# GpSimd computes half of the key-times-query products of the decode attention

## What is computed

```python
def diff_attn_sample(q, k_new, v_new, k_past, v_past, lam):
    ...
    s_past = jnp.einsum('bqhcd,bshcd->bhcqs', q, k_past, preferred_element_type=jnp.float32) * scale
    ...
    w = diff_combine(jnp.concatenate([s_past, s_new], axis=-1), lam).astype(v_new.dtype)
    return (jnp.einsum('bhqs,bshe->bqhe', w[..., :P], v_past)
            + jnp.einsum('bhqs,bshe->bqhe', w[..., P:], v_new))
```

## Time and profile before

| | us |
|---|---|
| median of 3 runs | 1510.65 |
| lowest and highest | 1507.95, 1510.95 |
| the profiled execution, its time | 1508.39 |
| its span in the profile | 1506.6 |
| attention stage, from the first key product of turn 0 to that of turn 7 and its end | 728.3 to 928.2, 956.8 |
| busy in the span: TensorE, VectorE, ScalarE, GpSimd | 1321.3, 858.7, 533.0, 21.3 |

### The profile page before, as it was taken

The page is one execution under the profiler, slowest core; times in us unless marked ns, Lnnn a source line. Parts: engine busy times, 40 slices in busy tenths (PEclk is TensorE's granted clock), DMA queues, the critical chain, the costliest instruction groups (busy, mean ns, idle before and its releaser), DMA issues.

```text
span 1506.6 us, 19271 instructions
## 1 busy us (share of the span) xinstructions
PE 1321.3 (88%) x7150; PEld 975.0 (65%) x7150; DVE 858.7 (57%) x1101; ACT 533.0 (35%) x613; POOL 21.3 (1%) x26
## 2 busy tenths in 40 slices
PE   4797788999999979898669988877898999999976
PEld 1795555888888866797223222236546888888864
DVE  1436553666666602745888999476506666666334
ACT  1433224555555503442111111122216555555321
POOL 2000010000000000000000000000100000000000
PEclk9899888999999988999757887979658999999988
DMA  9937612999999692555439878964006999999300
GB/s 335 386 126 291 223 56 91 351 335 335 338 334 335 228 376 72 193 187 180 168 132 339 305 270 310 327 215 167 1 0 244 337 341 332 342 337 341 122 2 29
DMA packets 143713, 355.32 MB, mean 236 GB/s; under 512 B 4706, under 2 KB 4899, under 8 KB 143652
## 3 DMA queue, kind: packets, MB, share of 16 engines
q1 hardware_dynamic: 142388, 350.91, 65.6%
q0 software_dynamic: 1264, 3.59, 0.8%
HBM read 351.20 MB, written 3.28 MB: 235 GB/s over the span
## 4 chain that ended last, share of the span: by engine, by line
PE 72%; DVE 18%; issue 4%; ACT 2%; SPq 2%; DMA 2%; ACTq 0%; POOL 0%; DVEq 0%
PE gu L615 23%; PE pj L386 20%; PE pj L634 15%; PE tb L420 4%; DVE wring L1791 4%; DVE tokB L1794 3%; PE tb L417 2%; PE gu L452 2%; PE pj L781 2%; DMA wring<-in_a_w_in 1%; SPq L878 1%; PE pj L486 1%; PE tb L558 1%; DVE wlo L1419 1%; DVE xT L1460 1%
## 5 line engine op out<-in xcount | busy, mean ns | idle before, releaser
L1646 DVE TENSOR_TENSOR wlo<-wring,whi 128x2048 fp32r<-128x2048 f32 x128 | 290.1, 2289 | 103.3 <-ACT whi L1198 103.3
L1198 ACT ACTIVATE whi<-wring 128x2048 fp32r<-128x2048 f32 x128 | 244.5, 1914 | 143.8 <-PE gu L615 143.8
L634 PEld LDWEIGHTS pj<-tokB,wring 128*128 128x128 f32 x2048 | 233.5, 192 | 4.8 <-issue 2.1
L634 PE MATMUL pj<-tokB,wring 128*128 128x128 f32 x2048 | 234.0, 275 | 1.7 <-issue 1.7
L615 PE MATMUL gu<-whi,xhi 128*128 128x512 f32 x512 | 207.2, 405 | 12.9 <-DVE xlo L1672 12.9
L1094 ACT ACTIVATE reg<-pj 128x264 f32<-128x264 f32 (+3 forms) x166 | 83.3, 509 | 365.0 <-PE pj L386 148.0
L615 PE MATMUL gu<-wlo,xhi 128*128 128x512 f32 x512 | 204.4, 399 | 0.0
L615 PE MATMUL gu<-whi,xlo 128*128 128x512 f32 x512 | 204.0, 398 | 0.0
L781 PE MATMUL pj<-wring,ws 128*8 128x512 f32 x256 | 127.7, 659 | 1.0 <-DVE lamx L1870 1.0
L615 PEld LDWEIGHTS gu<-whi,xhi 128*128 128x128 f32 x512 | 98.0, 191 | 36.0 <-DVE xlo L1672 7.9
L615 PEld LDWEIGHTS gu<-whi,xlo 128*128 128x128 f32 x512 | 97.9, 191 | 22.6
(11 more groups left out here) (288 smaller groups left out, 1711.9 us busy)
## 6 DMA issues: line engine op xcount, KB each, us to landing
wring<-in_moe_w_gate SPq DMA_DIRECT2D x32, 2048.0 KB, 9.1
wring<-in_moe_w_up SPq DMA_DIRECT2D x32, 2048.0 KB, 10.0
wring<-in_moe_w_down SPq DMA_DIRECT2D x32, 2048.0 KB, 9.1
wring<-in_ada_w SPq DMA_DIRECT2D x24, 2048.0 KB, 13.0
wring<-in_cache_k SPq DMA_DIRECT2D x64, 512.0 KB, 5.0
wring<-in_cache_v SPq DMA_DIRECT2D x64, 512.0 KB, 5.0
wring<-in_a_w_in SPq DMA_DIRECT2D x4, 2048.0 KB, 20.0
wring<-in_a_w_out SPq DMA_DIRECT2D x2, 2048.0 KB, 16.7
```

What stands on the lines that cost most here:

```text
L634: m = pe.matmul(bank[:, i * P:(i + 1) * P], w[:, k, f * P:(f + 1) * P], aT[:, k, :], start=(k == 0), stop=(k == FB - 1))
L1198: act.activation(whi[q], quarter(wring, q, s), ACT.Copy).then_inc(hi_ready, 1)
L1646: dve.tensor_tensor(quarter(wlo, q, s), quarter(wring, q, s), whi[q].bitcast(F32), ALU.subtract).then_inc(lo_ready, 1)
```

## The change

GpSimd gets a loop over the 8 sequences behind its last store. For each it waits until the query is spread, and then, for both slots k, until the slot is loaded; it multiplies the second half of the slot (pages 2 and 3 of the four) in place with the query and counts `product_ready`. VectorE no longer multiplies for q = 1; there it waits for `product_ready` and does the sum alone. Nothing else is changed: which slots are used, when they are given back, and the order on the other engines.

```diff
         keys_used = sem("keys_used")
+        product_ready = sem("product_ready")
...
             pool.dma_start(o["v_sample"].rearrange("b t h e -> (b t) (h e)"), tokA[0:NB, 2, :]).then_inc(stored["vs"], 16)
+            for s in range(NB):
+
+                pool.wait_ge(pj_evac, at[f"spread{s}"])
+                for k in range(2):
+                    slot, count = cache_slot("k", s, k)
+                    pool.wait_ge(slot_in[slot], at["cache_loads"][slot] + 16 * count)
+                    keys = wring[:, slot, 2 * D:4 * D].rearrange("p (g n) -> p g n", g=2)
+                    pool.tensor_tensor(keys, keys, qbc[:, s % 2:s % 2 + 1, :].to_broadcast([P, 2, D]),
+                                       ALU.mult).then_inc(product_ready, 1)
             clear(1)
...
                 keys = wring[:, slot, q * 2 * D:(q + 1) * 2 * D]
-                link(dve.tensor_tensor(keys.rearrange("p (g n) -> p g n", g=2), keys.rearrange("p (g n) -> p g n", g=2),
-                                       qbc[:, s % 2:s % 2 + 1, :].to_broadcast([P, 2, D]), ALU.mult))
+                if q == 0:
+                    link(dve.tensor_tensor(keys.rearrange("p (g n) -> p g n", g=2), keys.rearrange("p (g n) -> p g n", g=2),
+                                           qbc[:, s % 2:s % 2 + 1, :].to_broadcast([P, 2, D]), ALU.mult))
+                else:
+
+                    dve.wait_ge(product_ready, 2 * s + k + 1)
```

## The result

The changed kernel took 1529.08 us (median of 5 runs, 1519.17 to 1531.09) against 1510.65 before, 1.0123 times as long (95% interval 1.0102 to 1.0144).

The account below looks back on a forecast made before the run. TensorE bounds nearly all, VectorE the key-score stage. Turn 0 6.1 slower, turns 1, 2 to 6 and 7 faster by 3.4, 2.5 and 1.5: -1.3 from 1508.4, 1507.1; at the runs' median 1509 us, range 1485 to 1526.

Parts of the forecast that it names:

- the gain without contention: Whole stage, if GpSimd and VectorE cost each other nothing: 14.6 us faster, 1496; as a rival, chance 0.27.
- GpSimd's price of 4.4 us: Each GpSimd product of 2048 columns takes 4.4 us, the second operand read after the first; 2.2 kept as alternative.
- The two take turns: GpSimd products and VectorE steps with two SBUF inputs exclude each other; sums, PSUM reads and waits run beside; chance 0.52.
- Turn 0, +6.1: Four GpSimd products make VectorE wait 10.8 us, less 4.66 for two products taken away: 6.1 us slower.
- -3.4: Turn 1: 4.66 us won, less some 1.3 of wait as GpSimd still holds when turn 2 begins.
- Turn 7, -1.5: The last turn has no GpSimd product: 1.5 us faster.
- Turns 2 to 6, -0.5 each: GpSimd's wait uses up nearly all that VectorE wins: 0.5 us faster a turn, 2.5 in five.
- bound of +0.7 a turn: Slow end for turns 2 to 6: between 0.8 us faster and 0.7 slower a turn.
- Rival 2: Turns 2 to 6: one GpSimd product inside the softmax group, another ahead of VectorE's third product; 1535 or 1521; chance 0.18.
- +4 a turn: Rival 2's cost in turns 2 to 6: 8.8 us of waits, partly covered, some 4 left a turn, 20 in five.
- the clock on the winning side: Shorter waits might keep TensorE's clock up in turns 2 to 7, so that all 37.3 us could come: 1473.
- The range: Total time 1485 to 1526 us, leaving out the worse half of Rival 2 (0.09).

Follow-up runs that it names:

- e1: Changed kernel with GpSimd's products replaced by three memsets into an idle buffer, so it only writes; result not the reference's; 1493.5 us, ratio 0.9919.
- e5: e3 with GpSimd's second product released behind VectorE's second sum, so that it falls on the softmax group; 1503.5 us, ratio 0.997.
- e3: Changed kernel with GpSimd's products released only behind VectorE's own products; sequence 0's second slot stays with VectorE; 1496.25 us, ratio 0.9924.
- second trace: The changed kernel profiled again with no edit; 1529.16 us.
- first trace: The changed kernel's first profiled execution, no further edit; 1519.17 us, the shortest of its five runs.
- e8: Changed kernel with one more wait: GpSimd's second product of a pair waits until VectorE's third product has ended; 1499.8 us, ratio 0.9943.
- e7: Kernel before, VectorE doing all 32 products, with GpSimd copying 128x2048 into an idle buffer beside it, results unused; one run, 1514.7 us.

## Why the prediction was wrong, point by point

- **What bounds the kernel; what the gain without contention is.** Right. e1 gained 13.4 where 14.6 was worked out from the earlier trace rows.
- **GpSimd's price of 4.4 us.** Nearly right: 4.50 to 4.52 when alone. The Trainium skill (GPSIMD Engine Reference, Elementwise — side-by-side cycle accounting), with 4497 ns, was nearer still. The second operand's share is real: the same buffer twice takes 3.60, a copy 1.89.
- **The two take turns, whole instruction by whole instruction; sums, PSUM reads and waits don't.** Right as a rule. It was too narrow in one point: `TENSOR_SCALAR` steps are blocked as well, L1857 and, at a place where the prediction expected no contact, L1880.
- **Turn 0, +6.1.** Measured +4.8. The drawn-out steps sum nearly as forecast (1.97 + 4.36 + 4.27 = 10.6, of which 9.6 are waits, for 10.8), and turn 1 gave -4.7 where -3.4 was forecast: its second slot's product started at 786.06, behind turn 2's first product, and did not hold it up. Together +0.1 where +2.7 was forecast.
- **Turn 7, -1.5.** Measured -1.05.
- **Turns 2 to 6, -0.5 each: the step that failed.** It reads "GpSimd starts at about t = 12.5", and the second "at 19.3", from landings in the trace of before. But the page loads are issued when `keys_used` and the value reads free the slots, and the change moves that moment against the turn. SP's queue in the changed kernel, the key pages of turn 4 (start, us):

```profile
854.24 10.78 SPq L1008 DMA_DIRECT2D wring<-in_cache_k  x8
```

  They are issued from t = 0.6 on, against t = 3.2 before, and in the turns that became long GpSimd starts at t = 9.9 to 11.4 and 16.15 to 16.95. What had held SP back was the fourth sum of turn 3:

```profile
SPq L1008 <- DVE tokB L1808: 10.9, 1, 10.9
```

  That sum ended at 848.09, 5.6 us ahead of turn 4's start, because TensorE ends a long turn late; before, it ended 3.0 ahead (840.21, 843.20). In short turn 4 it ended 3.1 ahead, and turn 5's first product came at t = 13.0. In turn 5, where nothing held up VectorE, it ended 6.7 ahead, SP did not wait for it at all, and turn 6's first product came at t = 10.8. So a long turn and an undisturbed one both bring the next landings forward. The second half of the failure is feedback: the first product draws out the softmax group by 4.1 us (4.46 for 0.35), and so the group's end, or the third product, is still ahead when the second pages land. The prediction computed the first product's effect on VectorE, and put the second GpSimd product behind VectorE's third, without asking what happens if it comes 2 us sooner.
- **Its bound of +0.7 a turn was too tight for the same reason.** It stood for the forecast's own case, where one product is covered. e5 confirms that case: such turns cost +0.8 over e3, and in the changed kernel they are 0.6 to 0.9 shorter than before.
- **Rival 2 was the right mechanism**, with the right condition (two waits in one turn) and the right argument for it (a faster VectorE gives slots back earlier). It got 0.18, and "a later VectorE gives the slots back later" was held against it. That did not hold: in the second trace three long turns follow each other. After a long turn the first product came at t = 9.9 to 10.5 again (turn 4 of the first trace, turns 4 and 5 of the second).
- **Its price, +4 a turn, was too small.** A long turn cost 5.4 to 6.0. Missing was what TensorE does after standing 3.9 us for its transposes: its next 16 matmuls took 2.2 us more, and the stretch in which the first of them ran (840 to 846) has a granted clock of 0.54. The prediction had looked for the clock on the winning side alone.
- **Turn 2, +4.7, stood in no rival:** a product at the turn's uncovered end. Turns 2 to 6 sum to 4.7 + 6.0 - 0.6 - 0.9 + 5.4 = 14.6 in the best of five runs.
- **The range.** 1526 at the top lay 3 us short of the median. It stood for 17 us above the forecast; three long turns of 6 and turn 2's 4.7 are 22.7.

What stays open: how many of the long turns the typical execution has was seen in three traces only, and 2.6 of the 10.0 us between the first and second trace lie behind turn 6 and were not followed. Nor was it tried to fix the landing moments themselves, by other slots for the pages; e3 and e8 take their effect away instead. Turn 2 was long in all three traces, and what would keep it short was not tried by itself.

## What to carry to other kernels

Work moved to an engine that excludes another is not priced by its length but by what stands opposite while it runs. Find the stretches in which the other engine only sums, reads PSUM or waits, and release the moved work by a semaphore at their start, rather than by when its data happen to land. And when a change speeds up the consumer of a ring, take no landing moment from the trace of before: work it out again from the wait that releases the load, and ask at every step what happens if it comes one step earlier.

## What the runs showed of the hardware that I had not expected

- A VectorE step of 128 x 8 elements that takes 0.23 us takes 4.30 us if a GpSimd product has started 0.2 us ahead of it (L1880). GpSimd gets in at the gaps between small dependent steps; VectorE's long products hold it off in the same way (6.52 us for a product of 4.5).
- GpSimd's writing alone draws out VectorE's one-input `TENSOR_SCALAR` (1.49 us in e1 for 0.29, while a two-input step of the same size next to it kept its 0.35), and doesn't touch the two-input steps. Its reading, even of one input, blocks a two-input product (3.38 for 2.29 in e7).
- One program can have turns of 27.8 or 34.2 us at the same place, by less than 1 us in the landing of a transfer (GpSimd at t = 17.15 or 16.15), and its three traced executions took 1512.55, 1519.17 and 1529.16 us.
- TensorE's idle 3.9 us cost 6.1: the 16 matmuls behind it took 9.26 us where they took 7.03 otherwise, with a granted clock of 0.54 in the stretch in which the first of them ran (840 to 846).
